# Up products of wide entries with the weights stationary, in a layer of token mixers and 64 experts

## The reference, cut to what matters

```python
def _moe_ffn(h, router_w, router_bias, w1, w3, w2, ws1, ws3, ws2):
    ...                                    # 8 of 64 experts for each token, with weights wts
    def body(y, xs_b):
        rt, rw, e = xs_b                   # rows (tokens), their weights, the expert
        xb = h_pad[rt]
        hid = jax.nn.silu(xb @ w1[e]) * (xb @ w3[e])
        ob = (hid @ w2[e]) * rw[:, None]
        return y.at[rt].add(ob.astype(y.dtype)), None
```

## The kernel before, in words

| n | up products of the entry |
|---|---|
| to 64 | 8 pairs of strips (L1467) |
| 65 to 128 | 8 products of 512 columns (L1462) |
| 129 to 192 | 8 of 512 and 8 pairs of strips |
| above 192 | 16 of 512 |

## Time and profile before

### The profile page before, as it was taken

One profiled execution on the slowest core, in us unless ns is written; L12 is line 12 of the kernel. 1 busy time (PEld: TensorE's weight loads), 2 busy tenths in 40 slices (PEclk: granted clock), 3 DMA queues, 4 the chain that ended last, 5 costly groups with the idle time before them and its releaser, 6 DMA issues.

```text
span 2459.4 us, 32897 instructions
## 1 busy us (share of the span) xinstructions
PE 2400.4 (98%) x8544; PEld 1175.8 (48%) x8545; DVE 1179.6 (48%) x2744; ACT 482.6 (20%) x892; POOL 616.1 (25%) x628
## 2 busy tenths in 40 slices
PE   6999999999999999999999999999999999999997
PEld 3444444555544556665444455444444444444443
DVE  3377212666755666657335676443333333343332
ACT  3311000444432133333211112200000000000000
POOL 0000000000022100000211143555555545455441
PEclk9999999999999999999999999999999999999998
DMA  8132333443362333212433412599899999999995
GB/s 260 42 73 48 81 77 115 110 136 108 119 181 65 82 81 95 90 44 86 133 110 113 128 61 105 196 306 300 287 303 332 333 325 340 314 359 364 327 317 132
DMA packets 121190, 435.26 MB, mean 177 GB/s; under 512 B 21004, under 2 KB 23260, under 8 KB 95376
## 3 DMA queue, kind: packets, MB, share of 16 engines
q1 hardware_dynamic: 78208, 306.91, 35.8%
q0 software_dynamic: 42896, 127.25, 19.5%
HBM read 366.44 MB, written 71.70 MB: 178 GB/s over the span
## 4 chain that ended last, share of the span: by engine, by line
PE 89%; DVE 6%; DMA 1%; issue 1%; SPq 1%; ACT 1%; POOL 0%; DVEq 0%; POOLq 0%; ACTq 0%
PE psum L980 22%; PE psum L1462 17%; PE psum L1529 9%; PE psum L1065 8%; PE psum L1311 7%; PE psum L1467 5%; PE psum L1328 3%; PE psum L1268 2%; PE psum L1535 2%; PE psum L1372 2%; PE psum L1136 2%; PE psum L1146 2%; PE psum L1155 2%; PE psum L1395 1%; DMA mem<-in_ada_w 1%
## 5 line engine op out<-in xcount | busy, mean ns | idle before, releaser
L980 PE MATMUL psum<-mem 128*128 128x512 f32 x1536 | 690.2, 595 | 1.0 <-ACT mem L1656 1.0
L1462 PE MATMUL psum<-mem 128*128 x1008 | 449.9, 594 | 1.5 <-DVE mem L2673 1.0
L980 PEld LDWEIGHTS psum<-mem 128*128 128x128 f32 x1536 | 279.9, 191 | 294.4 <-issue 291.4
L785 POOL DMA_INDIRECT mem<-h_d,idx x287 | 293.7, 1023 | 354.6 <-DVE idx L2774 257.0
L1462 PEld LDWEIGHTS psum<-mem 128*128 128x128 f32 x1008 | 186.6, 190 | 229.6 <-issue 229.6
L2752 DVE TENSOR_TENSOR mem<-mem,psum 128x256 f32<-128x256 f32 x93 | 39.1, 421 | 419.0 <-ACT mem L1941 417.4
L1529 PE MATMUL psum<-mem 128*128 128x512 f32 x504 | 228.0, 599 | 1.0 <-issue 0.6
L1065 PE MATMUL psum<-mem 128*128 128x512 f32 x448 | 192.8, 592 | 0.0
L790 POOL DMA_INDIRECT out_x<-mem,put x93 | 140.5, 1510 | 99.0 <-issue 73.3
L1311 PE MATMUL psum<-mem 128*128 128x512 f32 x384 | 165.0, 592 | 0.0
L1529 PEld LDWEIGHTS psum<-mem 128*128 128x128 f32 x504 | 93.0, 190 | 124.6 <-issue 124.6
(11 more groups left out here) (421 smaller groups left out, 2488.4 us busy)
## 6 DMA issues: line engine op xcount, KB each, us to landing
mem<-in_exp_w SPq DMA_DIRECT2D x201, 1024.0 KB, 8.8
mem<-in_w_in SPq DMA_DIRECT2D x16, 2048.0 KB, 14.2
proj_d<-mem SPq DMA_DIRECT2D x104, 256.0 KB, 2.0
mem<-in_ada_w POOLq DMA_DIRECT2D x16, 1024.0 KB, 6.3
mem<-proj_d POOLq DMA_DIRECT2D x56, 256.0 KB, 3.0
mem<-proj_d POOLq DMA_DIRECT2D x20, 512.0 KB, 5.7
mem<-in_ada_w SPq DMA_DIRECT2D x4, 2048.0 KB, 23.0
mem<-in_w_branch SPq DMA_DIRECT2D x3, 2048.0 KB, 8.0
```

The lines of the kernel that those rows point to most:

```text
L785: g.indirect_dma_start(x[:, 2 * P * n:2 * P * (n + 1)], None, h2_q, bass.IndirectOffsetOnAxis(ap=idx[:, p, j, n:n + 1], axis=0), bounds_ch ...
L980: mm = t.matmul(bank(unit_bank(u)), l, r, start=(k == 0), stop=(k == KD - 1))
L1462: return t.matmul(bank(up_banks[j][r]), xgT[r][:, k, P * j:P * (j + 1)], up_piece(h, r, k), start=(k == 0), stop=(k == KD - 1))
```

## The change

For entries with n > 128 the roles of the operands are exchanged. 128 columns of w1 or w3 (those of one part f, read with a step of two) are stationary and n tokens, rounded up to 192 or 256, stream past (`up_wide`). The result has the hidden units on the partitions, so VectorE's multiply writes `hidT` directly, and these entries have no transposes and no copy. An entry then has four groups of 8 products: part 0 gate, part 0 value, part 1 gate, part 1 value. The first 15 products stand in `up_wide_begin`, ahead of the turn of the entry before, and the other 17 in `up_wide_end`. Entries up to 128 tokens are computed as before. The copy and turn semaphores become single ones with counters of their own (`turned`, `narrow`). TensorE's loop has one round more, and the tail is gone.

```diff
-        hid = [view(24064 + 256 * j, FF) for j in range(2)]
+        hid = view(24064, FF)
...
+            def up_wide(b, f, z, k, n):
+                w = w13[b][:, z, k, :].rearrange("p (n f) -> p f n", f=FK)[:, f, :]
+                return t.matmul(psum[:, up_banks[f][b % 2], 2 * P * z:2 * P * z + n], w, xgT[b % 2][:, k, 0:n],
+                                start=(k == 0), stop=(k == KD - 1))
...
+            def up_wide_begin(b, n):
                 for k in range(KD):
-                    mm = up_half(1, b, k)
+                    up_wide(b, 0, 0, k, n)
+                for k in range(KD - 1):
+                    up_wide(b, 0, 1, k, n)
+
+            def up_wide_end(b, n):
+                up_wide(b, 0, 1, KD - 1, n).then_inc(e_H[0], 1)
+                for z in range(2):
+                    for k in range(KD):
+                        mm = up_wide(b, 1, z, k, n)
                 mm.then_inc(e_H[1], 1)
 
+            def by_width(n, part, b):
+
+                with pe.If(n > P + HALF):
+                    part(b, 2 * P)
+                with pe.Else():
+                    part(b, P + HALF)
+                pe.nop()
+
             def up_begin(n, h, r):
 
                 with pe.If(n > HALF):
-                    for k in range(UP_AHEAD):
-                        up(0, h, r, k)
+                    with pe.If(n > P):
+                        with pe.If(h > 0):
+                            by_width(n, up_wide_begin, 2 + r)
+                        with pe.Else():
+                            by_width(n, up_wide_begin, r)
+                        pe.nop()
+                    with pe.Else():
+                        for k in range(UP_AHEAD):
+                            up(h, r, k)
+                    pe.nop()
...
             def up_end(n, h, r):
 
                 with pe.If(n > HALF):
-                    for k in range(UP_AHEAD, KD):
-                        mm = up(0, h, r, k)
-                    mm.then_inc(e_H[0], 1)
+                    with pe.If(n > P):
+                        seconds.up()
+                        with pe.If(h > 0):
+                            by_width(n, up_wide_end, 2 + r)
+                        with pe.Else():
+                            by_width(n, up_wide_end, r)
+                        pe.nop()
+                    with pe.Else():
+                        for k in range(UP_AHEAD, KD):
+                            mm = up(h, r, k)
+                        mm.then_inc(e_H[0], 1)
+                    pe.nop()
...
-                outs.wait(e_hc[1])
...
-                pe.wait_ge(e_hc[0], now)
                 with pe.If(n > HALF):
                     with pe.If(n > P):
                         down_second(n, p)
+                    with pe.Else():
+                        turned.wait(e_hc)
                     pe.nop()
...
                     with pe.If(n > P):
                         seconds.wait(e_hid[1])
-                        turn_tile(0)
-                        with pe.If(n > P + HALF):
-                            turn_tile(1)
-                        with pe.Else():
-                            turn_half_tile(1)
-                        pe.nop()
...
                 with pe.If(n > 0):
                     up_end(n, h, r)
-                    with pe.If(n > P):
-                        up_second(n, h, r)
-                    pe.nop()
...
-            with pe.Fori(0, NI // 4) as it:
+            with pe.Fori(0, NI // 4 + 1) as it:
...
-            with pe.If(pe.snap(n_last) > 0):
-                turn_hidden(pe.snap(n_last), NI + 1)
-                downs(pe.snap(n_last), 1, 16 * (NI // 2), NI + 1)
-            pe.nop()
...
-            def hidden(j, p):
-                v.tensor_tensor(hid[j], sg[:, j, :], bank(up_banks[j][p])[:, FF:2 * FF], ALU.mult).then_inc(e_hid[j], 1)
+            def hidden(dst, j, p):
+                v.tensor_tensor(dst, sg[:, j, :], bank(up_banks[j][p])[:, FF:2 * FF], ALU.mult).then_inc(e_hid[j], 1)
...
                 with dve.If(n > P):
+                    dve.wait_ge(e_si[0], now)
+                    hidden(hidT[p][:, 0, :], 0, p)
                     wide.up()
                     wide.wait(e_si[1])
-                    hidden(1, p)
+                    hidden(hidT[p][:, 1, :], 1, p)
+                with dve.Else():
+                    dve.wait_ge(e_si[0], now)
+                    hidden(hid, 0, p)
```

More of the change, by code:

```diff
@@ L342, in layer_kernel @@
         e_xg = [two("xg0"), two("xg1")]
-        e_H, e_si, e_hid, e_hT, e_hc, e_O, e_ob = (two(n) for n in ("H", "si", "hid", "hT", "hc", "O", "ob"))
+        e_H, e_si, e_hid, e_O, e_ob = (two(n) for n in ("H", "si", "hid", "O", "ob"))
+        e_hT, e_hc = sem("e_hT"), sem("e_hc")
         e_w += [sem(f"e_w{b}") for b in (2, 3)]
@@ L346, in layer_kernel @@
         e_T, e_red, e_idx, e_lists, e_sc, e_up = (sem("e_" + n) for n in ("T", "red", "idx", "lists", "sc", "up"))
-        to_clear = [*e_xg[0], *e_xg[1], *e_H, *e_si, *e_hid, *e_hT, *e_hc, *e_O, *e_ob,
+        to_clear = [*e_xg[0], *e_xg[1], *e_H, *e_si, *e_hid, e_hT, e_hc, *e_O, *e_ob,
                     e_T, e_red, e_idx, e_lists, e_sc, e_up, *e_w[2:], *e_v[2:]]
@@ L1450, in _ @@
             pe.wait_ge(e_clear, 1)
-            for x in (*e_H, *e_hT, *e_O):
+            for x in (*e_H, e_hT, *e_O):
                 pe.sem_inc(x, 1)
-            seconds, outs = Count(pe, "seconds"), Count(pe, "outs")
+            seconds, outs, turned = Count(pe, "seconds"), Count(pe, "outs"), Count(pe, "turned")
             n_now, n_last = pe.alloc_register("n_now"), pe.alloc_register("n_last")
@@ L1459, in up_piece, with up, up_half @@
                 return mem[:, bass.ds(2 * UP_N * h + UP_N * r, UP_N)].rearrange("p (w k f) -> p w k f", w=2, k=KD)[:, :, k, :]
-            def up(j, h, r, k):
-                return t.matmul(bank(up_banks[j][r]), xgT[r][:, k, P * j:P * (j + 1)], up_piece(h, r, k), start=(k == 0), stop=(k == KD - 1))
-            def up_half(j, b, k):
+            def up(h, r, k):
+                return t.matmul(bank(up_banks[0][r]), xgT[r][:, k, 0:P], up_piece(h, r, k), start=(k == 0), stop=(k == KD - 1))
+            def up_half(b, k):
@@ L1465, in up_half @@
                 w = w13[b][:, :, k, :].rearrange("p w (n f) -> p f w n", f=FK)
                 for f in range(FK):
-                    mm = t.matmul(psum[HALF * f:HALF * (f + 1), up_banks[j][b % 2], :].rearrange("p (w n) -> p w n", w=2)[:, :, 0:P],
-                                  xgT[b % 2][:, k, P * j:P * j + HALF], w[:, f, :, :], start=(k == 0), stop=(k == KD - 1))
-                return mm
+                    mm = t.matmul(psum[HALF * f:HALF * (f + 1), up_banks[0][b % 2], :].rearrange("p (w n) -> p w n", w=2)[:, :, 0:P],
+                                  xgT[b % 2][:, k, 0:HALF], w[:, f, :, :], start=(k == 0), stop=(k == KD - 1))
@@ L1508, in up_end @@
                         up_half_end(r)
-                    pe.nop()
-                pe.nop()
-            def up_second(n, h, r):
-                seconds.up()
-                with pe.If(n > P + HALF):
-                    for k in range(KD):
-                        mm = up(1, h, r, k)
-                    mm.then_inc(e_H[1], 1)
-                with pe.Else():
[L1520 to L1523, removed]
                     pe.nop()
@@ L1564, in downs, with turn_tile, turn_half_tile @@
                 pe.nop()
-            def turn_tile(j):
+            def turn_tile():
                 for f in range(FK):
[L1568 to L1572, removed]
+                    mm = t.transpose(psum[:, 1, f * P:(f + 1) * P], hid.rearrange("t (p f) -> t f p", f=FK)[:, f, :], ident[:, :])
+                mm.then_inc(e_hT, 1)
+            def turn_half_tile():
+                t.transpose(psum[:, 1, 0:P], hid[:, 0:P], ident[:, :]).then_inc(e_hT, 1)
             def turn_hidden(n, now):
@@ L1577, in turn_hidden @@
                         seconds.wait(e_hid[1])
-                        turn_tile(0)
-                        with pe.If(n > P + HALF):
-                            turn_tile(1)
-                        with pe.Else():
-                            turn_half_tile(1)
-                        pe.nop()
                     with pe.Else():
+                        turned.up()
                         pe.wait_ge(e_hid[0], now)
-                        turn_tile(0)
+                        turn_tile()
                     pe.nop()
                 with pe.Else():
+                    turned.up()
                     pe.wait_ge(e_hid[0], now)
-                    turn_half_tile(0)
+                    turn_half_tile()
                 pe.nop()
@@ L1941, in silu, with hidden_turned @@
                 s.activation(sg[:, j, :], bank(up_banks[j][p])[:, 0:FF], ACT.Silu).then_inc(e_si[j], 1)
-            def hidden_turned(j, p, n):
-                s.activation(hidT[p][:, :, P * j:P * j + n], psum[:, 1, FF * j:FF * j + 2 * n].rearrange("p (f n) -> p f n", f=FK), ACT.Copy).then_inc(e_hc[j], 1)
+            def hidden_turned(p, n):
```

(30 more changed lines are left out.)

7 lines of the change are left out of this document (2 added, 5 removed).

## The result

The changed kernel takes 2962.76 us (median of four runs, 2958.18 to 2971.72) against 2477.59 us for the kernel before (median of four). The ratio is 1.196, 95% interval [1.193, 1.199]. It is slower by a fifth, where 2460 us was forecast and the range ended at 2510.

A forecast was written before the change was run, and what follows sets the result against it. TensorE was taken to bound the expert loop. D gains 12.3 us, C 7.9, code costs 2: together -18, so 2443 on the profiled execution, 2460 us against the 2477.7 median; range 2450 to 2510.

The forecast's parts named there:

- The products: Up products of wide entries on TensorE: D 13.93 to 13.9 us, no change; C gains 0.2 us, seam included.
- The turning: Transposes of wide entries' hidden units, amid the next entry's products; removing them gains 0.95 us a D, 0.41 a C.
- A: Loop entry of up to 64 tokens; behind a D its products become one piece of 3.8 us instead of 4.81.
- D: Loop entry above 192 tokens, 13 of them; forecast gain 0.95 us each, 12.3 in all.
- B: Loop entry of 65 to 128 tokens; one of the four sizes.
- C: Loop entry of 129 to 192 tokens, 13 of them; forecast gain 0.2 + 0.41 us each, 7.9 in all.
- The stepped load: Rival: the wide products' two-element-step weight load sets TensorE's pace, C from 0.167 us a record; 2515 us at 0.222; chance 0.14.
- The transfers: Rival: DMA, share 0.97 mid-loop, cannot go faster, so TensorE waits for weights or tokens; 2475 us; chance 0.08.
- The extra round: One more loop round replaces a tail this run never enters; cost 0, under 1 us if TensorE were last.
- The first fetches: Bringing the larger loop code in during the first rounds, once; cost 2 us, range 0 to 8.

The follow-up runs named there:

- the kernel with the block: Changed kernel plus 28 never-executed products (112 instructions and a branch) ahead of the loop; 2465.34 us, ratio 0.9959 to the kernel before; again 2447.91 us, 0.9947.
- The kernel before with 85 dead products: Kernel before plus 85 never-executed products in each of the loop body's two entries (60 and 25); 2986.73 us against 2476.2, ratio 1.206.
- the one before with its block: Kernel before plus only 28 never-executed products ahead of the loop; 2460.94 us against 2461.3, ratio 1.000.
- 75 dead products: Kernel before plus 75 never-executed products in each of the loop body's two entries (50 and 25); 2473.83 us against 2461.3, ratio 1.0053.

## Why the prediction was wrong, point by point

**How the 500 us come about.** By the windows view the loop is 1358 us here and 845 in the kernel with the block, with the same 3401 records. Idle time of TensorE is 387 us against 10; busy time is 971 against 835, the clock being 0.85 against 1.00. So three quarters of the loss is waiting for code, and one quarter the lower clock that the waits bring with them. The kernel before with 85 dead products shows the same with no product changed: its loop has a clock of 0.87 and 1020.6 us of busy time, against 1.00 and 852.9 without them. The prediction had no term for the clock.

**The products** were right, and can be read in the kernel with the block (timeline of TensorE, for the earlier trace rows):

```profile
...
1710.07 5.04 PE L1474 MATMUL psum<-mem 128*128 128x192 f32 x30
1714.94 0.27 PE L1597 MATMUL psum<-ident,mem 128*128 128x128 f32 x1
1715.05 5.70 PE L1474 MATMUL psum<-mem 128*128 128x192 f32 x34
1720.68 1.94 PE L1559 MATMUL psum<-mem 128*64 128x512 f32 x8
1722.55 14.09 PE L1474 MATMUL psum<-mem 128*128 128x256 f32 x64
1736.56 1.94 PE L1559 MATMUL psum<-mem 128*64 128x512 f32 x8
```

An entry of 129 to 192 tokens takes 4.87 + 5.63 = 10.50 us (forecast 10.53; before 10.65). One above 192 takes 1722.55 to 1736.56, 14.01 (forecast 13.9; before 13.93). The records follow one another at 0.163 and 0.216 us, as forecast.

**The turning** goes as forecast, by sizes somewhat other than forecast: an A behind a D is one piece of about 3.8 us. From one D's down products to the next's, where a B is the third entry, it is 37.37 us against 38.09 where the copy is in time, and mostly 39.1 to 39.4 in the kernel before on the chips where it is late. From the first D's down products to the last product of all, the kernel with the block takes 767.4 us and the one before with its block 786.9 on the same chip. That is 19.6 us; the forecast was 20 for the whole loop. In part this is luck. By the starts of D's down products, the 8 D beside a B gained 0.77 us each, and the 4 beside a C 1.28 for the pair, so a C there about 0.5; the last 8 C, which follow the last D, gained 8.3 us, 1.04 each. The forecast had 0.95 for a D and 0.61 for a C, so D came out smaller, C larger, and the two misses cancel.

**The stepped load** (second rival) did not set the pace: 197 ns against 190. The 56 ns between transposes were no measure for it. **The transfers** (third rival) did not either: at 845 us for the loop the DMA share is 0.93, as it was before. **The extra round** cost nothing.

**The first fetches** were put at 2 us, range 0 to 8, and were more. The first entries of the kernel with the block:

```profile
...
1586.11 7.13 PE L1463 MATMUL psum<-mem 128*128 x16 [2.54 <-issue]
1596.62 4.55 PE L1463 MATMUL psum<-mem 128*128 x10 [3.39 <-issue]
1601.02 0.39 PE L1593 MATMUL psum<-ident,mem 128*128 128x128 f32 x2
1604.76 4.53 PE L1463 MATMUL psum<-mem 128*128 x6 [3.36 <-issue]
1609.13 3.17 PE L1553 MATMUL psum<-mem 128*128 128x512 f32 x7
```

TensorE stands idle for 2.54 and 3.39 us ahead of the first two groups of products and for 3.36 behind the first transposes; before it was 0.57, 0.96 and nothing. Up to the first D's down products it has lost 6.7 us to the kernel before with its block (1660.35 against 1653.68), although one C and one D are in that stretch; with their forecast gain the first fetches cost some 8 us. So 19.6 - 6.7 = 12.9 us, and 13.4 were measured. That is how the version with the block comes to 0.5% and not 0.8%.

## What to carry to other kernels

Variants of an inner loop that are written out (two widths times two buffers here) cost code, and more code in a loop costs little up to a step (12 us here for seven packets instead of five): on TensorE a loop whose packets and one more come to at most eight 16 KB packets (so seven of 256 instructions) stayed, one over eight packets was fetched again in every round, at some 15 us a round. Count the loop's instructions and the packet borders that it crosses before adding a variant; where a loop would fit into seven packets and lies over eight only because of where it starts, moving its start is enough, as 112 instructions that never run did here. In a profile the sign is "issue" waits of TensorE with no releaser, branches of microseconds, and a queue of instruction packets that never ends.

## What the runs showed of the hardware that was not expected

- The step: 20 products (80 instructions) of code that never runs, fewer or more, are 2473.8 against 2986.7 us, each beside a kernel before of 2461 and 2476.
- Waits for code bring the clock down: 0.85 granted over the loop, 136 us of the loss.
- A stepped float32 weight load is recorded at 197 ns, an unstepped one at 190; between the transposes of the earlier trace rows the difference is 56 ns.
- The first rounds of a loop over 7 packets show 7 to 9 us of "issue" waits of TensorE ahead of 1620 us (7.0 with 75 dead products, 9.3 in the kernel with the block); in the kernel before, such waits are 0.6 us there.
- In the kernel with the block on a slower chip, five records in the first entry above 192 tokens came one by one, 0.7 to 2.1 us apart (1645.01 to 1650.99), with no instruction packet between them; no run here tells why.
- The same kernel differs by 16 us (0.65%) between chips. In the kernel before, 11 us of it are waits of TensorE for a copy of ScalarE; the kernel with the block has no such waits and differs by 17 us.
